# Modulation sums of a two-block network: VectorE's fused multiply-add against a ScalarE scaling and a POOL add

## The reference, cut to what matters

```
mod = silu(c) @ w_ada + b_ada                   # 2048 x 12288
sh_m, sc_m, gt_m, sh_f, sc_f, gt_f = split(mod, 6)
h = rmsnorm(x) * (1 + sc_m) + sh_m
proj = h @ w_in                                 # 2048 x 8208
y = concat(hgrn2(proj[:, :4096]), gated_delta(proj[:, 4096:])) @ w_out
x = x + gt_m * rmsnorm(y)
h = rmsnorm(x) * (1 + sc_f) + sh_f              # then the FFN, gated by gt_f
```

## Time and profile before

| what | us |
|---|---|
| median of 3 runs | 2801.17 |
| lowest and highest | 2796.95, 2801.18 |
| profiled execution | 2805.43 |
| span of its profile | 2803.6 |
| TensorE busy | 2688.6 |
| VectorE busy | 1889.5 |
| ScalarE busy | 1247.7 |
| POOL busy | 22.9 |

### The profile page before, as it was taken

One profiled execution on the slowest core, in us unless ns is written; L12 is line 12 of the kernel. 1 busy time (PEld: TensorE's weight loads), 2 busy tenths in 40 slices (PEclk: granted clock), 3 DMA queues, 4 the chain that ended last, 5 costly groups with the idle time before them and its releaser, 6 DMA issues.

```text
span 2803.6 us, 36490 instructions
## 1 busy us (share of the span) xinstructions
PE 2688.6 (96%) x13470; PEld 2191.0 (78%) x13470; DVE 1889.5 (67%) x2148; ACT 1247.7 (45%) x1418; POOL 22.9 (1%) x12
## 2 busy tenths in 40 slices
PE   3899999999799999999989999999999999999998
PEld 2478777778688888888867888888888888888887
DVE  6779796897666666666666556555557666666667
ACT  2153443554444444444444554444454444444444
POOL 0000000000000000000000000000000000000000
PEclk9899999999899999999999999999999999999999
DMA  9988776867566666666636446665556666666664
GB/s 350 341 233 273 215 259 208 205 209 254 185 220 204 220 204 217 209 216 218 204 123 183 143 136 210 195 193 193 194 179 194 189 187 187 187 187 187 188 189 161
DMA packets 281415, 578.27 MB, mean 206 GB/s; under 512 B 19658, under 2 KB 20452, under 8 KB 280164
## 3 DMA queue, kind: packets, MB, share of 16 engines
q1 hardware_dynamic: 273492, 560.13, 63.5%
q10 hardware_dynamic: 7824, 16.78, 1.6%
HBM read 574.75 MB, written 2.10 MB: 206 GB/s over the span
## 4 chain that ended last, share of the span: by engine, by line
PE 86%; DVE 6%; DMA 5%; ACT 2%; issue 2%; SPq 0%; ACTq 0%; DVEq 0%
PE bank L474 26%; PE bank L475 26%; PE bank L479 26%; DMA early<-in_w_ada 4%; PE bank L756 3%; PE bank L753 3%; DMA raw<-in_w_in 1%; DVE w_lo L464 1%; DVE acc L1961 1%; DVE gd_t L2326 1%; DVE gd_t L1924 1%; PE bank L1168 0%; ACT w_hi L459 0%; DVE acc_w L1961 0%; PE bank L492 0%
## 5 line engine op out<-in xcount | busy, mean ns | idle before, releaser
L464 DVE TENSOR_TENSOR w_lo<-raw,w_hi 128x1024 fp32r<-128x1024 f32 x860 | 1050.5, 1229 | 651.4 <-ACT w_hi L459 648.7
L459 ACT ACTIVATE w_hi<-raw 128x1024 fp32r<-128x1024 f32 x860 | 911.1, 1061 | 1211.3 <-PE bank L479 1067.2
L474 PE MATMUL bank<-w_hi,op_a_hi 128*128 128x512 f32 x2192 | 873.9, 399 | 1.7 <-issue 1.7
L475 PE MATMUL bank<-w_hi,op_a_lo 128*128 128x512 f32 x2192 | 858.9, 392 | 0.0
L479 PE MATMUL bank<-w_lo,op_a_hi 128*128 128x512 f32 x2192 | 589.3, 391 | 2.2 <-DVE w_lo L464 2.1
L474 PEld LDWEIGHTS bank<-w_hi,op_a_hi 128*128 128x128 f32 x2192 | 415.2, 189 | 91.4 <-issue 5.9
L479 PEld LDWEIGHTS bank<-w_lo,op_a_hi 128*128 128x128 f32 x2192 | 413.0, 189 | 90.2 <-DVE w_lo L464 3.5
L475 PEld LDWEIGHTS bank<-w_hi,op_a_lo 128*128 128x128 f32 x2192 | 415.3, 189 | 83.8 <-issue 1.2
L474 PE MATMUL bank<-w_hi,hid_hi 128*128 128x512 f32 x832 | 326.5, 392 | 0.0
L475 PE MATMUL bank<-w_hi,hid_lo 128*128 128x512 f32 x832 | 323.9, 389 | 0.0
L479 PE MATMUL bank<-w_lo,hid_hi 128*128 128x512 f32 x832 | 222.7, 389 | 0.0
(11 more groups left out here) (257 smaller groups left out, 1924.5 us busy)
## 6 DMA issues: line engine op xcount, KB each, us to landing
raw<-in_w_ff SPq DMA_DIRECT2D x256, 512.0 KB, 3.7
raw<-in_w_in SPq DMA_DIRECT2D x244, 512.0 KB, 4.6
raw<-in_ffn_w_up SPq DMA_DIRECT2D x176, 512.0 KB, 3.7
ada_raw<-in_w_ada SPq DMA_DIRECT2D x96, 512.0 KB, 6.6
raw<-in_ffn_w_down SPq DMA_DIRECT2D x88, 512.0 KB, 4.4
early<-in_w_ada SPq DMA_DIRECT2D x26, 1024.0 KB, 13.6
raw<-in_w_out SPq DMA_DIRECT2D x32, 512.0 KB, 5.0
ada_raw_f<-in_w_ada SPq DMA_DIRECT2D x32, 512.0 KB, 4.5
```

The lines of the kernel that those rows point to most:

```text
L459: nc.scalar.activation(w_hi[:, gj % RAW], raw[:, j % RAW], ACT.Copy).then_inc(hi_ready, 1)
L464: nc.vector.tensor_tensor(w_lo[:, gj % RAW], raw[:, j % RAW], w_hi[:, gj % RAW].bitcast(F32), ALU.subtract).then_inc(lo_ready, 1)
L474: nc.tensor.matmul(where[:, t], hi(kt + k, tok), w_hi[:, s, k], start=first and k == 0, stop=False)
L475: nc.tensor.matmul(where[:, t], lo(kt + k, tok), w_hi[:, s, k], start=False, stop=False)
```

## The change

`add_woven_ada` leaves VectorE. ScalarE now waits for the landed piece and multiplies it in place by its column of `c_act`, in step n, right after `split_hi` of piece n+3. POOL waits for that (`ada_scaled`), and for the add of the piece before the last, and adds the piece to `acc_w`; the first piece of a half is copied, after a wait that keeps the copy behind the earlier readers of `acc_w`. The buffer is released (`ada_used`) by POOL. To free a semaphore for `ada_scaled`, "lab" is merged into "bb". The loads and their order are as before.

```diff
--- before.py
+++ after.py
@@ -369,6 +369,7 @@
         early_landed = [sem(f"early_landed{n}") for n in range(EARLY)]
         xt_ready = sem("xt_ready")
         ada_used = sem("ada_used")
+        ada_scaled = sem("ada_scaled")
         hi_ready = sem("hi_ready")
         lo_ready = sem("lo_ready")
         w_used = sem("w_used")
@@ -399,7 +400,7 @@
             "ge", "sq", "ss", "rs", "on", "o", "hi", "lo")}
         gd = {n: sem("gd_" + n) for n in (
             "ab_hi", "ab_lo", "abt", "ab", "bf", "tap", "z", "ez", "lz", "eb", "ea", "la", "g", "eg", "conv", "silu", "sq", "lnp", "ln",
-            "lab", "bb", "gc", "d", "ge", "ke", "ktl", "kb", "kk", "qk", "qde", "qd", "kg", "vb", "ct", "x", "xx", "p",
+            "bb", "gc", "d", "ge", "ke", "ktl", "kb", "kk", "qk", "qde", "qd", "kg", "vb", "ct", "x", "xx", "p",
             "u", "wt", "s1", "vn", "gte", "osq", "ss", "rs", "on", "o", "hi", "lo")}
         gt_ready = sem("gt_ready")
         ff = {n: sem("ff_" + n) for n in ("act", "made", "hi", "lo")}
@@ -887,10 +888,10 @@
                 yield
                 yield
                 yield
-                W("lab")
+                W("bb", 1, 2)
                 units(T("grow"), lambda u, o: turned(o, XT[:, u]), gd["gc"], g + 1)
                 yield
-                W("bb")
+                W("bb", 2, 2)
                 units(T("beta"), lambda u, o: turned(o, PP[:, u]), gd["kb"], g + 1)
                 yield
                 yield
@@ -1658,6 +1659,9 @@
             for n in range(STEPS):
                 if n + 3 > EARLY_DONE:
                     split_hi(act, 0, n + 3, 0, n + 3)
+                for k in ADA_AT[n]:
+                    act.wait_ge(ada_landed[k % 3], 16 * (k // 3) + 16)
+                    f(ada_raw[k % 3][:], ada_raw[k % 3][:], ACT.Copy, ada_scaled, scale=c_act[:, k % (2 * KT) // 2:k % (2 * KT) // 2 + 1])
                 if n in (21, 23, 25):
                     keep((n - 21) // 2)
                 if n % KP == 1 and 3 * KP < n <= GEMM["out"] + KP and n // KP - 1 >= 3:
@@ -1960,14 +1964,6 @@
                 else:
                     v.scalar_tensor_tensor(out=dst, in0=src, scalar=kt, in1=dst, op0=ALU.mult, op1=ALU.add).then_inc(ada_used, 1)
 
-            def add_woven_ada(k):
-
-                kt, h = k % (2 * KT) // 2, k % 2
-                dve.wait_ge(ada_landed[k % 3], 16 * (k // 3) + 16)
-                if kt:
-                    dve.wait_ge(ada_used, ADA_BASE + k - 1)
-                add_ada(c_act[:, kt:kt + 1], ada_raw[k % 3][:], acc_w[:, 2 * CH * h:2 * CH * (h + 1)], kt == 0)
-
             def newton(k, r=None, done=None):
 
                 if not k:
@@ -2331,7 +2327,7 @@
                     ins.then_inc(gd["conv"], 1)
                     yield
                 yield
-                v.tensor_copy(jt(XT), over4(g_cum)).then_inc(gd["lab"], 1)
+                v.tensor_copy(jt(XT), over4(g_cum)).then_inc(gd["bb"], 1)
                 v.tensor_copy(jt(PP), over4(beta)).then_inc(gd["bb"], 1)
                 yield
                 W("silu", 1, 3)
@@ -2460,8 +2456,6 @@
             for n in range(STEPS):
                 if n + 2 >= EARLY_DONE:
                     split_lo(dve, 0, n + 2, n + 2)
-                for k in ADA_AT[n]:
-                    add_woven_ada(k)
                 c = n - GEMM["out"] - 5
                 if c >= 16 and c % 4 == 0:
                     add_out(c // 4)
@@ -2885,6 +2879,26 @@
 
             p.memset(rows[:], 0.0).then_inc(zeroed, 1)
 
+            def add_woven_ada(n, k):
+
+                kt, h = k % (2 * KT) // 2, k % 2
+                pool.wait_ge(ada_scaled, k + 1)
+                dst, src = acc_w[:, 2 * CH * h:2 * CH * (h + 1)], ada_raw[k % 3][:]
+                if kt:
+                    pool.wait_ge(ada_used, ADA_BASE + k - 1)
+                    p.tensor_tensor(dst, dst, src, ALU.add).then_inc(ada_used, 1)
+                    return
+                if k < 2 * KT:
+                    pool.wait_ge(lo_ready, rounded(n + 2))
+                    pool.wait_ge(op_hi, 4)
+                else:
+                    pool.wait_ge(made, TILE[(f"gdn{k // (2 * KT) - 1}", 0, "mod5")] + 1)
+                p.tensor_copy(dst, src).then_inc(ada_used, 1)
+
+            for n in range(STEPS):
+                for k in ADA_AT[n]:
+                    add_woven_ada(n, k)
+
             pool.wait_ge(hg["lo"], GROUPS)
             p.memset(Y[:], 0.0).then_inc(zeroed, 1)
 
```

## The result

| | before | after |
|---|---|---|
| median, us (4 runs each, same chip) | 2799.7 | 2883.24 |
| profiled execution | 2805.43 | 2881.56 |
| span of its profile | 2803.6 | 2879.7 |
| TensorE busy | 2688.6 | 2714.2 |

The ratio is 1.0296 [1.0284, 1.0308]: slower by 83 us. Sign and kind were as forecast, the size was not, and the time lies outside the range. Rows of the kernel after are one line number later in the weight splits (460 for 459, 465 for 464) and the loads (511, 637).

The account below looks back on a forecast made before the run. TensorE, busy 96%, was taken as the bound, with late weight loads as second limit. Terms 24.8 + 12.3 + 2.0 - 3.7 + 4 = +39.4 on 2805.4 gave 2844.8, less 4.3 for the median: 2840 us, range 2812 to 2866.

Parts of the forecast that it names:

- the loop of split, scaling, add and load: Thick modulation stretches: each weight load stands behind POOL's add, closing a loop every two weight pieces, against TensorE's nine us.
- the sum of the link: One turn of the load loop: split 0.96, scaling 1.06, semaphore 0.03, add 2.8, issue 0.40, landing 5.2: 10.5 us.
- the second group: From the split of piece 87 at 404.90 us: three double links, column sums at 452.5 instead of 440.23, +12.3 us.
- the signs that the prediction set itself: POOL adds 2.4 to 3.4 us, longer ScalarE load waits, SyncE waiting on adds, TensorE idle some 10 us before column sums.
- The sign set down as "partly wrong": VectorE's w_lo subtraction stretched far beyond 1.23 us, with TensorE waiting for it, would point to the shared port.
- the chain: Weight loads wait behind POOL's add, which follows ScalarE's scaling and split; column sums come late by 24.8 and 12.3 us.
- I count no gain, since ScalarE and the shared port take back what VectorE gains: TensorE's idle 1.85 + 1.73 us in the two thick stretches: no gain from VectorE's relief, range -3.6 to +3.6.
- The port rival: The port VectorE shares with POOL binds in the thick stretches, not the load chain: 2821 us, chance 0.17.
- the TensorE stalls ... behind late weight loads, should go: -3.7: After each column sum POOL takes late pieces at once, removing stalls of 1.2 us (300 to 320) and 2.5 us (460 to 480).
- the first group: From the split of piece 40 at 208.47 us: eight links, 89.6 us; column sums at 307.9 instead of 283.11, +24.8.
- the stretch of the gate sums: Gate sums at 671.74 us wait for piece 95, scaled after a late split, until 673.7: +2.0 us.
- the clock, +4: Long TensorE stalls before the column sums lower the granted clock: 2 us for each group, 0 to 8 as ends.

Follow-up runs that it names:

- e5: The changed kernel with ScalarE scaling the modulation pieces ahead of its weight split in each step, not behind it: 2830.75 us, 1.0102.
- e7: The changed kernel with modulation loads issued from POOL's own queue, right behind the add that frees the buffer: 2833.54 us, 1.0116.
- e13: The changed kernel with a fourth ada_raw buffer for the first 60 pieces: 2851.74 us, 1.0186.
- e2: The changed kernel with ScalarE scaling only 128 of the 1024 columns of each piece; POOL adds whole pieces: 2882.4 us, 1.0278.
- e6: e5 with POOL adding only 128 of the 1024 columns of each piece (sums incomplete): 2791.33 us, 0.9969.
- e11: The changed kernel with scaling ahead of the split and VectorE adding the scaled pieces in place of POOL: 2808.15 us, 1.003.
- e14: e5 with a fourth ada_raw buffer for the first 60 pieces: 2829.3 us, 1.0103.
- e10: e5 and e7 together, scaling ahead of the split and modulation loads from POOL's queue: 2839.19 us, 1.0134.
- e9: e6 with a full POOL add on a scratch tile behind each step's adds, for 64 of the 96 pieces: 2804.55 us, 1.0012.
- e12: The changed kernel with filler multiplications on TensorE in four of its long waits: 2880.84 us, 1.0287.

## Why the prediction was right in kind and half in size

**Right.** The mechanism of the forecast: the loop of split, scaling, add and load lost the lead of the splits, and e5, e7 and e13 undo it for 52, 50 and 31 us. The add was priced at 2.8 us and took 2.74; the scaling at 1.06 and took 1.14. At the late links the scaling runs beside the w_lo of the same piece, and the add ends some 2.2 us behind that w_lo (e2); the sum of the link, which had the port in its price for the add, came out nearly the same: 4.85 us forecast from the split to the end of the add, 4.5 at pieces 54 to 56. In the second group, from the split of piece 87 to the column sums, 47.6 us were forecast and 46.5 measured (448.8 to 495.31). ScalarE's added work costs nothing by itself (e6, e11).

Of the signs that the prediction set itself, the price of the adds and SyncE's wait for them came true. ScalarE's wait for weight loads was to rise well above 107.8 us and reached 116.9; TensorE was to stand idle for some 10 us ahead of both column sums and stood 6.6 and 4.9. The sign set down as "partly wrong" came as well: w_lo was stretched, to 1.61 us. TensorE does not wait for w_lo itself (1.0 us in all), but for VectorE's other work in the recurrences.

By cause, with the two orders: the chain was forecast at 39 us, all of the sum, and cost 52 (2883 less 2831); VectorE's side was forecast at nothing and cost 31 (2831 less 2800: 40 for the long add, less 9 of relief). By place the miss (37 us between the profiled executions, 44 by medians) is spread over the whole stretch, as the list by steps shows.

**Failed: "I count no gain, since ScalarE and the shared port take back what VectorE gains".** This term, 0 within 3.6 us, is the largest miss, 31 us. POOL's adds take back more than VectorE gained, 40 us against 9. The port rival (+20) was weighed as an alternative to the chain, because "the links are longer"; the table of the two orders shows that they add: with the loads freed, 30 us remain. That the 30 are the port's is shown in part. They do not come from late weight loads: ScalarE waits 29.9 us for those in e5, 24.8 in e14 and 5.8 in e10, and the time does not fall. They do not come from the sums either, for which TensorE waits 0.7 us in e5. It waits for VectorE, and VectorE's instructions are longer. e9 puts POOL's work on another tile, where nothing waits for it, and still loses 13 of the 40 us between e6 and e5, with 64 of 96 pieces and shorter adds; w_lo goes to 1.50 us (1.69 in e5), the twelve operations of the recurrence on the table only to 1.12 (1.96 in e5). Over steps 36 to 92, where both have a full-width add for each piece, the profiled e9 is 10 us behind e6 and 13 ahead of e5. So about half of the other 27 us is not the last 32 pieces; whether it is those twelve and their like, which the dummies hit less, or the place of the long add in the ring was not separated.

**Failed: "the TensorE stalls ... behind late weight loads, should go: -3.7".** Instead the late pieces added 8 and 7 us. The count link by link was ended at the column sums, but the lead had been used up there, and the pieces behind them run the same loop (the rows at 334 to 345 us). The stage's copies on ScalarE were named as queued behind and priced at nothing; they are where TensorE meets the late loads, not a cost of their own: in e5, with the same copies, it waits 4.5 us for them instead of 29.9.

**Mis-sized: the first group.** Its eight links took 97.4 us instead of 89.6. One of them met POOL's adds on VectorE: VectorE was late with a product for TensorE (the stall of 5.24 us at 226.63), and steps 36 to 42 lost 8 us in which no column sum was near. The same steps lose 6 us in e5 and 7 in e9, and 1 in e6, whose adds are short. The stages before the gate sums (+5 instead of 0) and the stretch of the gate sums (+9 instead of 2) make up the last 12 us; no run tried them apart.

**Not the missing term: the clock, +4.** TensorE was busy for 25.6 us more, part of it at half clock behind its stalls, and this looked like the missing term. e12 took away about half of what the mean clock had lost and gained 2.4 us, within the intervals. That fits the reading that a slow TensorE only fills time that it would have waited, while the loop sets the pace; the other half, with the stretch behind the second column sums, was not tried.

## What to carry to other kernels

Before moving an operation to another engine, list what the new engine's instruction stands behind, and follow the buffer that it frees to the loads queued behind its refill: here the place of the same 1 us of scaling, behind a split or ahead of it, was worth 52 us (e5). Ask what the new engine's work does to the instructions of the old one: here the adds on POOL made VectorE's subtractions and products longer, and that price came on top of the chain's. Where a lead is used up, go on counting links beyond the point at which the first stall shows.

## What the runs showed that was not expected

VectorE's plain copies are held as well, and for nearly a whole POOL add. One copy in the kernel before, then timelines of the kernel after, VectorE and POOL:

```profile
208.27 0.69 DVE L2334 COPY gd_t<-gsm 128x1024 f32<-128x1024 f32 x1
```

```profile
203.18 2.91 DVE L2330 COPY gd_t<-gsm 128x1024 f32<-128x1024 f32 x1
206.01 2.89 DVE L2331 COPY gd_t<-gsm 128x1024 f32<-128x1024 f32 x1
...
203.13 2.41 POOL L2889 TENSOR_TENSOR acc_w<-acc_w,ada_raw 128x1024 f32<-128x1024 f32 x1 [31.16 <-ACT ada_raw L1323]
...
205.49 2.86 POOL L2889 TENSOR_TENSOR acc_w<-acc_w,ada_raw 128x1024 f32<-128x1024 f32 x1
```

The same two copies took 0.69 us each before. Here the first begins 0.05 us behind the first add, the second 0.52 behind the second, and each ends 0.55 us behind its add. The prediction had taken from the earlier trace rows that both engines wait for parts of an instruction only. Those rows say the same as these: the POOL add of 3.34 us ends 2.26 us behind the w_lo that was running when it began, and the w_lo of 1.85 us ends 1.08 behind that add, each a little less than it takes alone (2.40 and 1.23). So in these rows the engine that came later waited for the rest of the other's instruction; it was a part only because it came late. The Trainium skill's "SBUF — State Buffer", section "Who interferes with whom", counts copies among the VectorE operations that can take the shared pair of ports, and lets the later engine wait for a whole instruction: the rows of the two copies agree.
